# Block 0 of a two-part transformer kernel: input products from part products, paired attention scores and values, probabilities turned by a diagonal

## The chip, the core and the metric

The program runs on one core of one Trainium2 chip. The metric is the device time of one execution in microseconds, the median of several; lower is better. The engines are TensorE (PE in the profile, its weight loads PEld), VectorE (DVE), ScalarE (ACT), GpSimd (POOL) and SyncE (SP), which issues most DMAs. Each works through its own queue in order and waits on semaphores.

## The reference

256 tokens of width 1024 go through two blocks with a mixture of experts each, and then through a second model part (gated linear and forgetting attention, cross attention, MLP). All is float32. The change lies in block 0, before its experts:

```python
m   = ada_mod(c, ada_w[0], ada_b[0])                     # six vectors of 1024: silu(c) @ w + b
hn  = modulate(rms_norm(h, norm1_g[0]), m0, m1)          # latent rows, 256 x 1024
hcn = modulate(rms_norm(ctx, norm1_g[0]), mc0, mc1)      # context rows
proj = hn @ w_in                                         # 512 q | 128 k | 128 v | 512 u | 512 gate
q, k = rms_norm per head (64), rope;   v                 # 8 query heads, 2 key-value heads
k, v = concat(context k, v from hcn @ w_in[:, 512:768], own k, v)      # 512 keys
p    = softmax(q k^T / 8);   attn = p v                  # in blocks of 128 queries
g    = silu(layer_norm(depthwise_conv31(u * sigmoid(gate)) + b))
h    = h + m2 * (concat(attn, g) @ w_out)
```

Then the router of block 0 picks 32 tokens for each of 16 experts and the experts' weights (96 chunks of 2 MB) are streamed.

## The kernel before

**The ring.** All large weights pass through one ring of nine slots of 2 MB in SBUF, filled by SyncE in the order of `STREAM`. `load(i, ...)` (line 470) waits until chunk i-9 is used up, then issues the DMA. TensorE counts `chunks_used`. The order at the start is ada0a (4 chunks), u, gate, q, kv, ada0b, ada0c, ada1a, ada1b, ada1c (4 each), ev_out (2), then the experts. `arrived` waits for a chunk's DMA.

**Orders are written by hand.** Each engine has a function with its instructions in program order; what runs between what is fixed there. The numbers `TAPS_Q, TAPS_KV, TAPS_LOOP` and `LN_AT` say how many of the 124 convolution taps (31 taps on 4 channel groups) VectorE does in each place, and at which head the layer norm steps stand.

**Input products.** `transposes("x")` and `transposed` give the modulated input as columns xT. TensorE then multiplies in plain float32: u and gate to columns (`to_columns`, lines 1915 to 1922), q to rows (`to_rows`, 1907), the context is transposed, own and context k/v to rows (`kv_rows`, 2004). VectorE does gating, taps, context columns, then the norms of heads and rope (1305 to 1347). `ada(g, c, bank)` (1860 to 1873) multiplies one chunk of modulation weights, four narrow products side by side; group 1 stands before the attention, groups 2 to 5 inside its loop.

**Attention.** For each of 16 (block, head) pairs: `ev_scores` (2051), two ahead; VectorE takes the negated maximum; ScalarE the exponential with its sum; `ev_transposed` (2059) turns four 128x128 pieces by transposes; VectorE (even heads) or ScalarE (odd) copies them to SBUF as pT; `ev_values` (2066) multiplies pT, as the stationary operand, by 64 columns of values. `attn_rows` (1353) divides a block by its sums, and eight transposes (2112) turn the result to columns. `cv_sums` (2075), `ln_center`, `ln_inverse` and `ln_scale` are the layer norm of the convolution.

**Part products.** From ev_out on the kernel multiplies by parts: ScalarE rounds an operand to float32r (hi), VectorE or GpSimd subtracts (lo = x - hi), and `split_product` (1924) adds three products:

```python
for n, (x, y) in enumerate(((0, 1), (1, 0), (0, 0))):
    last = mm(out, lhs[x], rhs[y], start=start and n == 0, stop=stop and n == 2)
```

`ev_high` and `ev_low` make the halves of the ev_out chunks, through two buffers `evw_hi`. `low` (line 460) does it later in the kernel on either engine. `add_gated` adds the product to h, and `route` begins.

Of the kernel before, what the change touches and what calls it, by code (L numbers as in the profile page):

```python
# [5 lines left out]
F32 = mybir.dt.float32  # L6
# [6 lines left out]
P = 128  # L13
D = 1024
# [59 lines left out]
STREAM = [("ada0a", 4), ("ev_u", 1), ("ev_gate", 1), ("ev_q", 1), ("ev_kv", 1), ("ada0b", 4),  # L74
# [46 lines left out]
def build(nc, a):  # L121
    ctx = ExitStack()
    with ctx:
# [50 lines left out]
        def at(off, **dims):  # L174
# [5 lines left out]
            if len(dims) == 1:  # L180
# [9 lines left out]
        vall = at(7168, t=4, e=128)  # L190
# [4 lines left out]
        cwrow = at(8824, d=512)  # L195
# [4 lines left out]
        sq = rows_t[:, 0:1280].rearrange("p (t h e) -> p t h e", t=NT, h=10)  # L200
        sq_ctx = rows_t[:, 1280:1536].rearrange("p (t h e) -> p t h e", t=NT, h=2)
        ra, rb, rc, rd = (rows_t[:, 320 * j:320 * (j + 1)].rearrange("p (h e) -> p h e", h=10) for j in range(4))
# [4 lines left out]
        attn = xT_t[:, 0:1024].rearrange("p (t e) -> p t e", t=NT)  # L207
# [72 lines left out]

        evw_hi = [rows_hi.rearrange("p k n -> p (k n)"), parts_of("scratch", SLOT // 2, 5632)]
        ev_x = [[parts_of("scratch", 4 * N, first).rearrange("p (k n) -> p k n", k=4) for first in pair]
                for pair in ((1536, 7680), (2560, 3584))]
# [89 lines left out]
        SPLIT_INPUTS = ["ev_out", "mix1", "y", "mix2", "w_out", "xattn", "wo", "mlp"]  # L373
        NORM_BANKS = {n: (4, 5, 6, 7) for n in TRANSPOSED}
        NORM_BANKS["moe0"], NORM_BANKS["moe1"] = (4, 5, 2, 3), (0, 1, 2, 3)
# [24 lines left out]
        LN_AT = 10  # L400
        TAPS_Q, TAPS_KV, TAPS_LOOP = 35, 12, 8
# [33 lines left out]

        def ev_half(j, p):

            i, s = FIRST["ev_out"] + j, slice(SLOT // 2 * (1 - p), SLOT // 2 * (2 - p))
            return 2 * j + p, ring[:, slot_of(i), s], ring_r[slot_of(i)][:, s], evw_hi[p]
# [26 lines left out]
        def _(sp):  # L466
# [47 lines left out]
            sp.dma_start(ctx_rows, a["ctx"][0].rearrange("(t p) d -> p t d", p=P)).then_inc(sem("ctx_in"), 16)  # L514
            columns("ev_kv", evw, 1, width=256, col0=512)
            for g in range(1, len(ADA)):
                modulations(g)
# [40 lines left out]
        def _(act):  # L558
# [7 lines left out]
            act.wait_ge(sem("c_ps"), 1)  # L566
# [59 lines left out]

            act.wait_ge(sem("x_in"), 16)
# [8 lines left out]
            act.wait_ge(sem("ctx_in"), 16)  # L636
            squares("ctx", ctx_rows, by_token(flat(cT)))
# [4 lines left out]
            whole(act, "ev_gate")  # L642
            for j in range(2):
                nc.scalar.activation(flat(sg[:, 2 * j:2 * j + 2, :]), pb(6 + j), ACT.Sigmoid).then_inc(sem("cv_gate"), 1)

            whole(act, "ev_q")
# [5 lines left out]
            transposed("ctx", cT)  # L652
            for w, bank in ((0, 2), (1, 3)):
                if w:
                    whole(act, "ev_kv")
                else:
                    act.wait_ge(sem("own_kv"), 1)
# [6 lines left out]
                if not w:  # L664
                    act.wait_ge(sem("inverses"), 1)
# [10 lines left out]
            def ev_probs_T(m):  # L676
                act.wait_ge(sem("ev_pT_ps"), m + 1)
                if m >= 2:
                    act.wait_ge(sem("ev_pv"), m - 1)
                nc.scalar.activation(flat(pT[:, 1]), pb(5), ACT.Copy).then_inc(sem("ev_pT_act"), 1)  # L680

            for n in range(NT * NQ):
# [8 lines left out]
                if n == LN_AT:  # L691
                    act.wait_ge(sem("cv_centered"), 1)
                    nc.scalar.activation(flat(csq), flat(cacc), ACT.Square).then_inc(sem("cv_sq"), 1)
                if n == LN_AT + 1:
                    act.wait_ge(sem("inverses"), 3)
                    nc.scalar.activation(lnrow[:, :], lnrow[:, :], ACT.Sqrt).then_inc(sem("roots"), 1)
            ev_probs_T(NT * NQ - 1)
            def ev_high(j, p):

                n, w, lo, hi = ev_half(j, p)  # L700
# [1962 lines left out]
```

## Time and profile before

| | us |
|---|---|
| median of 3 runs (lowest, highest) | 1674.82 (1673.35, 1675.28) |
| the profiled execution, its own time | 1671.44 |
| its span (first to last instruction) | 1669.6 |
| PE busy | 1471.2 (88%) |
| DVE busy | 481.2 (29%) |
| ACT busy | 339.5 (20%) |
| POOL busy | 110.6 (7%) |

The granted TensorE clock is 0.966 of full speed over the span. HBM delivers 337 GB/s in the mean over the span, and 410 to 430 GB/s where the DMA engines are busy all the time. The rows below come from views of the profile: tables of stretches with the busy time of each engine, timelines (merged runs of equal instructions in order of time), groups of equal instructions, and lists of the durations of one line. Durations of TensorE instructions overlap, so the distance from one start to the next is the price of one, and the last one adds its tail.

### The profile page before, as it was taken

How to read it: one execution, taken by the hardware profiler on the slowest of the kernel's cores; microseconds unless marked ns; L12 is line 12 of the kernel's file. 1: busy time of each engine (PE TensorE's matmuls, PEld its weight loads, DVE VectorE, ACT ScalarE, POOL GpSimd, SP SyncE). 2: the span in 40 equal slices, each digit the busy share in tenths (PEclk: the TensorE clock that was granted, in tenths of full speed). 3: DMA queues.
4: the chain of work that ended last, by engine and by line, in shares of the span. 5: the costliest groups of instructions: out<-in, count | busy, mean ns of one | idle time of the engine just before them, and what ended most of it. 6: DMA issues, size and time to landing. Idle time of an engine off the chain costs nothing. (4 is left out here: it accounts for less than half of the span.)

```text
span 1669.6 us, 17591 instructions
## 1 busy us (share of the span) xinstructions
PE 1471.2 (88%) x7708; PEld 824.5 (49%) x7708; DVE 481.2 (29%) x732; ACT 339.5 (20%) x515; POOL 110.6 (7%) x109
## 2 busy tenths in 40 slices
PE   4999979889888899789798878978888999999999
PEld 2755642232232343289532323323324767788897
DVE  1496540100100000156500001001004754345443
ACT  1122410000000000143200000000003645544442
POOL 0000000000000000010000000000003044330000
PEclk9999989999989999999799999999999999999999
DMA  9989959999999999996399999999999844244510
GB/s 374 410 359 413 410 216 429 414 429 427 416 428 427 412 428 429 407 398 234 126 418 422 427 430 419 429 427 423 428 424 355 291 175 149 104 148 168 189 51 26
DMA packets 93298, 563.06 MB, mean 337 GB/s; under 512 B 8048, under 2 KB 9448, under 8 KB 53670
## 3 DMA queue, kind: packets, MB, share of 16 engines
q1 hardware_dynamic: 89504, 551.77, 81.2%
q0 software_dynamic: 2384, 9.42, 1.6%
q8 instruction: 61, 1.00, 0.2%
q10 hardware_dynamic: 1334, 0.75, 0.2%
q14 instruction: 15, 0.12, 0.0%
HBM read 558.74 MB, written 3.17 MB: 337 GB/s over the span
## 5 line engine op out<-in xcount | busy, mean ns | idle before, releaser
L2207 PE MATMUL ps<-ring,scratch 128*32 128x512 f32 x2048 | 434.6, 610 | 54.4 <-DMA ring<-in_moe_w_up 26.1
L2207 PEld LDWEIGHTS ps<-ring,scratch 128*32 128x32 f32 x2048 | 129.2, 112 | 346.7 <-issue 339.5
L2186 PE MATMUL ps<-ring,scratch 128*32 128x512 f32 x1024 | 205.8, 603 | 29.7 <-DMA ring<-in_moe_w_down 29.7
L1927 PE MATMUL ps<-ring_parts,scratch_parts 128*128 128x512 f32 x656 | 186.6, 402 | 5.0 <-DVE xT_parts L1189 1.4
L1927 PE MATMUL ps<-scratch_parts,ring_parts 128*128 128x256 f32 x704 | 146.0, 282 | 0.0
L1927 PEld LDWEIGHTS ps<-ring_parts,scratch_parts 128*128 128x128 f32 x656 | 122.4, 189 | 33.1 <-DVE xT_parts L1189 1.6
L2186 PEld LDWEIGHTS ps<-ring,scratch 128*32 128x32 f32 x1024 | 50.3, 111 | 160.8 <-issue 107.8
L607 ACT ACTIVATE ring_parts<-ring 128x2048 fp32r<-128x2048 f32 x56 | 106.4, 1919 | 93.1 <-PE ps L1927 86.6
L460 DVE TENSOR_TENSOR ring_parts<-ring,ring_parts 128x2048 fp32r<-128x2048 f32 x46 | 105.6, 2296 | 54.9 <-ACT ring_parts L607 53.8
L1927 PEld LDWEIGHTS ps<-scratch_parts,ring_parts 128*128 128x128 f32 x704 | 114.7, 189 | 0.3
L1519 DVE TENSOR_TENSOR scratch<-ps,gate_bc 128x512 f32<-128x512 f32 x16 | 11.1, 692 | 250.9 <-PE ps L2186 250.9
L1927 PE MATMUL ps<-xT_parts,ring_parts 128*128 128x256 f32 x288 | 80.5, 280 | 1.3 <-DVE xT_parts L1180 1.3
L2215 PE MATMUL ps<-scratch,rows 128*128 128x128 f32 x256 | 66.5, 421 | 13.1 <-DVE scratch L1548 5.6
L2215 PEld LDWEIGHTS ps<-scratch,rows 128*128 128x128 f32 x256 | 61.6, 327 | 31.2 <-issue 15.4
L1508 DVE TENSOR_TENSOR scratch<-scratch,ps 128x1024 f32<-128x1024 f32 x8 | 9.8, 1222 | 231.4 <-PE ps L2207 231.4
L1912 PE MATMUL ps<-ring,xT 128*128 128x512 f32 x160 | 72.9, 617 | 2.2 <-DVE xT L1168 2.2
L742 ACT ACTIVATE scratch<-ps,mod_cols,scale_cols 128x128 f32<-128x128 f32 x32 | 12.9, 453 | 277.8 <-PE ps L2215 277.8
L1927 PE MATMUL ps<-ring_parts,xT_parts 128*128 128x512 f32 x160 | 62.6, 391 | 0.0
L1504 DVE SCALAR_TENSOR_TENSOR scratch<-ps,cst,scratch 128x256 f32<-128x256 f32 x8 | 3.9, 484 | 188.2 <-ACT scratch L746 188.2
L1872 PE MATMUL ps<-ring,silu_c 128*32 128x512 f32 x384 | 49.3, 648 | 7.7 <-issue 6.8
L1927 PEld LDWEIGHTS ps<-xT_parts,ring_parts 128*128 128x128 f32 x288 | 54.6, 190 | 1.8 <-issue 1.5
L754 ACT ACTIVATE scratch<-ps 128x512 f32<-128x512 f32 x8 | 4.8, 597 | 245.7 <-PE ps L2241 245.7
(393 smaller groups left out, 1552.1 us busy)
## 6 DMA issues: line engine op xcount, KB each, us to landing
ring<-in_moe_w_gate SPq DMA_DIRECT2D x64, 2048.0 KB, 30.0
ring<-in_moe_w_up SPq DMA_DIRECT2D x64, 2048.0 KB, 17.9
ring<-in_moe_w_down SPq DMA_DIRECT2D x64, 2048.0 KB, 30.1
ring<-in_ada_w SPq DMA_DIRECT2D x24, 2048.0 KB, 15.3
ring<-in_mlp_w SPq DMA_DIRECT2D x16, 2048.0 KB, 8.7
ring<-in_sc_w_in SPq DMA_DIRECT2D x6, 2048.0 KB, 21.5
ring<-in_w_in SPq DMA_DIRECT2D x6, 2048.0 KB, 20.7
ring<-in_xattn_wkv SPq DMA_DIRECT2D x4, 2048.0 KB, 35.5
```

What stands on the lines that cost most here:

```text
L460: ops.tensor_tensor(lo, w, hi.bitcast(F32), ALU.subtract).then_inc(sem("w_split"), 1)
L607: nc.scalar.activation(hi, w, ACT.Copy).then_inc(sem("w_high"), 1)
L742: last = nc.scalar.activation(xsT[:, k, :], ps[:, GATHER[b], P * (k % 2):P * (k % 2 + 1)], ACT.Identity, scale=scale[:, k:k + 1], bias=shi ...
L754: nc.scalar.activation(flat(hT[:, 4:8, :]), pb(7), ACT.Copy).then_inc(sem("mo_hT_act"), 1)
L1508: nc.vector.tensor_tensor(hid, hid, ps[:, 2:4, :].rearrange("p b f -> p (b f)"), ALU.mult)\
L1519: nc.vector.tensor_tensor(ym[:, 512 * j:512 * j + 512], pb(4 + j), gate_bc[:, 512 * j:512 * j + 512], ALU.mult).then_inc(sem("mo_ym"), 1)
L1872: last = mm(ps[32 * j:32 * j + 32, bank, :], lhs, rhs, start=(c == k == 0), stop=(c == 3 and k == 1))
L1912: last = mm(ps[:, banks[t], col:col + width], lhs[:, k, P * t:P * (t + 1)], slot8(i)[:, k, 0:width], start=(k == 0), stop=(k == KD - 1))
L1927: last = mm(out, lhs[x], rhs[y], start=start and n == 0, stop=stop and n == 2)
L2186: last = mm(ps[32 * j:32 * j + 32, banks[half], :], src[:, k, CAP * j:CAP * (j + 1)], w[:, e, col:col + 512], start=(k == 0), stop=(k == K ...
L2207: last = mm(ps[32 * j:32 * j + 32, banks[half], :], src[:, k, CAP * j:CAP * (j + 1)], w[e][:, 0, col:col + 512], start=(k == 0), stop=(k = ...
L2215: last = mm(ps[:, GATHER[b], P * (k % 2):P * (k % 2 + 1)], run_slice(rows[:, t, :], k), onehot[:, t, P * g:P * (g + 1)], start=(t == 0), s ...
```

## The change

It works on block 0 before the experts alone. In words:

- u, gate, q and kv are multiplied by parts, in seven halves (`IN_HALVES`), each rounded by ScalarE (`in_high`) and subtracted by GpSimd (halves 0, 3, 4, 5, 6) or VectorE (1, 2). x and the context columns are split too, the context by GpSimd. u and gate go alternately by halves, so the first two channel groups of the convolution start after two halves; the taps are done by pairs of groups.
- kv comes after ada0b in the stream. ada group 2 is multiplied before the attention.
- Scores of two heads stand next to each other, on different row halves of the array. Probabilities are multiplied by a diagonal of the inverse sums instead of transposed, which turns and divides in one. Values are the stationary operand (64 columns) and pT the moving one; two heads go to different column halves, and the result is already in columns. `attn_rows` and the eight transposes go.
- The layer norm steps and the ev_out halves get new places; the half that multiplies the attention comes first.

```diff
-STREAM = [("ada0a", 4), ("ev_u", 1), ("ev_gate", 1), ("ev_q", 1), ("ev_kv", 1), ("ada0b", 4),
+STREAM = [("ada0a", 4), ("ev_u", 1), ("ev_gate", 1), ("ev_q", 1), ("ada0b", 4), ("ev_kv", 1),
...
-        LN_AT = 10
-        TAPS_Q, TAPS_KV, TAPS_LOOP = 35, 12, 8
+        TAPS_FIRST, TAPS_Q, TAPS_KV, TAPS_LOOP = 40, 26, 12, 7
+        MEAN_AT, CENTER_AT, SQUARE_AT, VAR_AT, ROOT_AT, SCALE_AT = 7, 8, 9, 12, 13, 14
+        ATTN_HIGH_AT, ATTN_LOW_AT, EV_HIGH_AT = 10, 11, 14
+        EV_HALVES = [(0, 1), (1, 1), (0, 0), (1, 0)]
+        IN_HALVES = [("ev_u", 0), ("ev_gate", 0), ("ev_u", 1), ("ev_gate", 1), ("ev_q", 0), ("ev_q", 1), ("ev_kv", 0)]
...
+        def in_low(eng, ops, n):
+            w, lo, hi = in_half(n)
+            eng.wait_ge(sem("in_high"), n + 1)
+            if n:
+                eng.wait_ge(sem("in_low"), n)
+            ops.tensor_tensor(lo, w, hi.bitcast(F32), ALU.subtract).then_inc(sem("in_low"), 1)
...  ScalarE
             squares("x", h, xT_rows)
+            in_high(0)
             transposed("x", xT)
+            pairs_high("x", xT, in_hi)
+            in_high(1)
...
+            in_high(2)
...
+            gates(0)
+            in_high(3)
+            in_high(4)
+            gates(1)
+            in_high(5)
+            in_high(6)
...  GpSimd
             rms("x")
+            in_low(pool, nc.gpsimd, 0)
             rms("ctx")
+            for n in range(3, len(IN_HALVES)):
+                in_low(pool, nc.gpsimd, n)
+            for b in range(4):
+                c = slice(2 * b, 2 * b + 2)
+                pool.wait_ge(sem("x_high"), 4 * SPLIT_INPUTS.index("ctx") + b + 1)
+                nc.gpsimd.tensor_tensor(in_hi[:, c, :], cT[:, c, :], xT_r[:, c, :].bitcast(F32), ALU.subtract)\
+                    .then_inc(sem("x_split"), 1)
...  VectorE, before the head norms
+            gated(0)
...
+            taps(TAPS_FIRST)
+            gated(1)
+            normed("ctx", ctx_rows, ctx_rows)
             dve.wait_ge(sem("gpad"), 2)
             taps(TAPS_Q)
+            in_done(dve, 6)
             transposed("ctx", cT)
-            taps(TAPS_KV)
...  VectorE, in the loop over heads
+            def weighted(n):
+                dve.wait_ge(sem("ev_p"), n + 1)
+                if n >= 2:
+                    dve.wait_ge(sem("ev_pT_ps"), n - 1)
+                link(nc.vector.reciprocal(sm[:, 112 + n:113 + n], sm[:, 96 + n:97 + n]))
+                nc.vector.tensor_scalar(diag[:, n % 2, :], ident, sm[:, 112 + n:113 + n], None, ALU.mult)\
+                    .then_inc(sem("ev_diag"), 1)
...
-                taps(TAPS_LOOP)
+                taps(3)
+                weighted(n)
+                taps(TAPS_LOOP - 3)
...  TensorE
+            half_used(in_columns(0, 4))
+            half_used(in_columns(1, 6))
...
+            used(in_columns(2, 5))
+            used(in_columns(3, 7))
+            pe.wait_ge(sem("norm_ss"), 4)
+            half_used(in_rows(4))
+            used(in_rows(5))
             pe.wait_ge(sem("gpad"), 2)
             pe.wait_ge(sem("cv_gate"), 2)
             transposes("ctx", ctx_rows)
...
+            half_used(kv_rows(2, (in_hi, xT_r)))
             for c in range(4):
                 ada(1, c, 3)
+            pe.wait_ge(sem("ev_rows"), 2)
+            input_split("ctx")
+            used(kv_rows(0, (xT_r, in_hi)))
+            for c in range(4):
+                ada(2, c, 7)
...
                 for s in range(4):
-                    last = nc.tensor.transpose(ps[:, 4 + n % 2, P * s:P * (s + 1)], pexp[:, n % 2, P * s:P * (s + 1)], ident)
+                    last = mm(ps[:, 4 + n % 2, P * s:P * (s + 1)], pexp[:, n % 2, P * s:P * (s + 1)], diag[:, n % 2, :],
+                              start=True, stop=True)
...
                 for s in range(4):
-                    last = mm(ps[:, 6 + t, 64 * (n % 8):64 * (n % 8) + 64], pT[:, w, s, :], vall[:, s, 64 * w:64 * w + 64],
-                              start=(s == 0), stop=(s == 3))
+                    for m in (n, n + 1):
+                        t, i, w = ev_head(m)
+                        o, k = 64 * (i % 2), 2 * w + i // 2
+                        last = mm(ps[o:o + 64, 6 + t, P * k:P * (k + 1)], vall[:, s, 64 * w:64 * w + 64], pT[:, w, s, :],
+                                  start=(s == 0), stop=(s == 3))
...
             for n in range(NT * NQ):
                 ev_transposed(n)
+                if n % 2 == 0:
+                    if n + 2 < NT * NQ:
+                        ev_scores(n + 2)
+                        ev_scores(n + 3)
+                    if n:
+                        ev_values(n - 2)
...
+                if n == MEAN_AT:
+                    cv_sums(0)
+                if n == VAR_AT:
+                    cv_sums(1)
```

## Rows read from the trace of the kernel before

**Rows 1.** Table of stretches: length, busy us (instructions) per engine, PE clock, DMA share, GB/s
```profile
240.00:260.00 20.00, 19.06 (x104) 7.49 (x105) 0.73 (x2) 0.81 (x2) 0.00 (x0) 1.00 1.00 425
220.00:240.00 20.00, 11.43 (x59) 7.01 (x59) 10.79 (x30) 1.50 (x6) 0.00 (x0) 0.74 0.40 120
191.00:213.50 22.50, 22.50 (x100) 18.16 (x99) 12.37 (x14) 5.47 (x5) 0.00 (x0) 1.00 0.79 319
```

**Rows 2.** Timeline of TensorE: start us, length us, what; one product is two instructions
```profile
36.76 14.05 PE L1920 MATMUL ps<-xT,ring 128*128 128x256 f32 x64 [2.65 <-ACT xT L592]
...
95.36 3.64 PE L1872 MATMUL ps<-ring,silu_c 128*32 128x512 f32 x32 [0.88 <-ACT scratch L663]
```

**Rows 3.** Timeline of TensorE in the attention
```profile
105.62 1.95 PE L2056 MATMUL ps<-scratch 64*128 64x512 f32 x6 [0.40 <-DVE scratch L1351]
...
136.62 0.66 PE L2064 MATMUL ps<-cst,scratch 128*128 128x128 f32 x4
137.11 1.00 PE L2071 MATMUL ps<-scratch 128*128 128x64 f32 x8
...
140.76 1.12 PE L2056 MATMUL ps<-scratch 64*128 64x512 f32 x2
...
163.43 1.95 PE L2084 MATMUL ps<-scratch,ones 128*128 128x256 f32 x8
...
170.22 0.66 PE L2064 MATMUL ps<-cst,scratch 128*128 128x128 f32 x4 [0.22 <-ACT scratch L686]
...
187.91 1.09 PE L2112 MATMUL ps<-cst,xT 128*128 128x128 f32 x8 [1.08 <-DVE xT L1359]
```

**Rows 4.** Timeline of TensorE, part products of 256 columns late in the kernel
```profile
1285.35 0.28 PE L1927 MATMUL ps<-xT_parts,ring_parts 128*128 128x256 f32 x1
...
1285.70 0.28 PE L1927 MATMUL ps<-xT_parts,ring_parts 128*128 128x256 f32 x1
```

**Rows 5.** Line 470, issue of the u chunk: ns min/median/max, start; landing after it
```profile
L470 SPq DMA_DIRECT2D ring<-in_ev_w_in x1: 3916/3916/3916, 7.1 to 7.1; - x1
...
DMA to landing us min/median/max: 27.0/27.0/27.0
```

**Rows 6.** Timeline of ScalarE, a rounding
```profile
181.91 1.90 ACT L706 ACTIVATE rows_parts<-ring 128x2048 fp32r<-128x2048 f32 x1
```

**Rows 7.** Subtractions by line: ns min/median/max, first and last start us
```profile
L460 DVE TENSOR_TENSOR ring_parts<-ring,ring_parts x46: 2229/2292/2595, 1277.4 to 1650.7; 128x2048 fp32r<-128x2048 f32 x46
L460 POOL TENSOR_TENSOR ring_parts<-ring,ring_parts x10: 4558/4578/4623, 1385.9 to 1477.8; 128x2048 fp32r<-128x2048 f32 x10
...
L1607 DVE TENSOR_TENSOR xT_parts<-xT,scratch_parts x4: 678/680/1780, 712.7 to 715.6; 128x512 fp32r<-128x512 f32 x4
```

**Rows 8.** Timeline of VectorE: taps, squares of the head norms, squares for the context
```profile
68.65 12.35 DVE L1294 SCALAR_TENSOR_TENSOR scratch<-scratch 128x256 f32<-128x256 f32 x31
...
88.43 1.49 DVE L1313 TENSOR_TENSOR rows<-scratch 128x1280 f32<-128x1280 f32 x1 [0.87 <-ACT scratch L663]
...
100.71 0.42 DVE L1313 TENSOR_TENSOR rows<-scratch 128x256 f32<-128x256 f32 x1
```

**Rows 9.** Timeline of GpSimd around two meetings with VectorE
```profile
709.36 4.52 POOL L1071 TENSOR_TENSOR ring_parts<-ring,scratch_parts 128x2048 fp32r<-128x2048 f32 x1 [0.93 <-DVE rows L1155]
...
1284.53 1.44 POOL L1030 TENSOR_TENSOR rstd<-ms,mhalf 128x1 f32<-128x1 f32 x1
```

**Rows 10.** Timeline of VectorE at the same two places
```profile
712.65 1.78 DVE L1607 TENSOR_TENSOR xT_parts<-xT,scratch_parts 128x512 fp32r<-128x512 f32 x1 [0.93 <-ACT scratch_parts L823]
...
1284.28 1.28 DVE L1650 SCALAR_TENSOR_TENSOR h<-h,rstd,scratch 128x1024 f32<-128x1024 f32 x1 [1.45 <-POOL rstd L1030]
```

**Rows 11.** Groups by form: busy us, mean ns of one, idle before
```profile
L2375 PE MATMUL ps<-scratch 64*128 64x128 f32 x16 | 1.2, 285 | 0.0
...
L2354 PE MATMUL ps<-cst,ms 128*128 128x128 f32 x4 | 0.6, 273 | 0.0
```

**Rows 12.** Table of stretches, one us in the attention's start
```profile
114.00:115.00 1.00, 1.00 (x8) 0.20 (x4) 1.00 (x4) 0.00 (x0) 0.00 (x0) 0.50 0.95 397
```

More of the change, by code:

```diff
@@ L194, in build @@
         cw = at(9848, c=CT, j=34)
-        cwrow = at(8824, d=512)
+        cwrow = at(9336, d=512)
         grow = at(9336, i=P)
@@ L1276, in _, with gated @@
             link(nc.vector.memset(gpad[:, :, edge + N:PADW], 0.0))
-            whole(dve, "ev_u")
-            for j in range(2):
+            def gated(j):
+                in_done(dve, (0, 2)[j])
                 dve.wait_ge(sem("cv_gate"), j + 1)
@@ L1419, in _ @@
-            ev_low(0, 1)
-            mod_cols(5, 3)
-            nc.vector.tensor_copy(router_bias, ps[:, 2, 0:E])
+            ev_low(0, 1)
+            attn_low(1)
+            ev_low(1, 1)
+            dve.wait_ge(sem("mo_shift"), 1)
+            nc.vector.tensor_copy(router_bias, ps[:, 2, 0:E])
+            ev_low(0, 0)
+            for b in range(2):
+                hi, lo = (flat(v[:, 2 * b:2 * b + 2, :]) for v in ev_x[0])
+                dve.wait_ge(sem("x_high"), 4 * SPLIT_INPUTS.index("ev_out") + 2 + b + 1)
+                nc.vector.tensor_tensor(lo, flat(cacc[:, 2 * b:2 * b + 2, :]), hi.bitcast(F32), ALU.subtract)\
+                    .then_inc(sem("x_split"), 1)
@@ L1914, in to_rows @@
                 return last
-            def to_columns(i, rhs, banks):
-                for c in range(4):
-                    for k in range(KD):
-                        last = mm(ps[:, banks[c // 2], N * (c % 2):N * (c % 2 + 1)], slot8(i)[:, k, P * c:P * (c + 1)],
-                                  rhs[:, k, :], start=(k == 0), stop=(k == KD - 1))
-                return last
             def split_product(out, lhs, rhs, start, stop):
@@ new lines, in in_rows @@
+            def in_rows(n):
+                w, lo, hi = in_half(n)
+                pe.wait_ge(sem("in_low"), n + 1)
+                half = IN_HALVES[n][1]
+                for t in range(NT):
+                    s = slice(P * t, P * (t + 1))
+                    for kk in range(4):
+                        k, c = 4 * half + kk, slice(512 * kk, 512 * kk + 512)
+                        last = split_product(pb(t), (in_hi[:, k, s], xT_r[:, k, s]), (hi[:, c], lo[:, c]), k == 0, k == KD - 1)
+                return last
@@ new lines, in _, with ev_product @@
+            ev_values(NT * NQ - 2)
+            def ev_product(j, p, t):
+                n, w, lo, hi = ev_half(j, p)
+                pe.wait_ge(sem("w_split"), n + 1)
+                s = slice(P * t, P * (t + 1))
+                for k in range(4):
+                    c = slice(512 * k, 512 * k + 512)
+                    if p or k % 2 == 0:
+                        input_split("ev_out", t if p else 2 + k // 2)
+                    last = split_product(pb(((0, 1), (4, 5))[j][t]), (ev_x[p][0][:, k, s], ev_x[p][1][:, k, s]),
+                                         (hi[:, c], lo[:, c]), p == 1 and k == 0, p == 0 and k == 3)
+                return last
```

326 lines of the change are left out of this document (170 added, 156 removed).

## Prediction

> **What bounds the kernel now.** I read the table of stretches first, then the timelines of TensorE, VectorE, ScalarE and GpSimd in block 0, then single groups for the prices. Weights stream through a ring of nine slots. From 240 us on the DMA engines are busy all the time and move 425 GB/s, but from 220 to 240 only 0.40 of it [rows 1]: the ring is full and TensorE has not yet reached the first experts. So the end of block 0 sets when the stream goes on, and each microsecond that TensorE reaches the experts later or earlier goes unshortened to the end. Until then TensorE is nearly always busy: input products from 36.8 us, the next ada group at 95.4, attention until 186.8, the ev_out product from 191.0 to 213.5 [rows 1 to 3]. The forecast is the shift of that last number. It is made on the profiled execution (span 1669.6, own time 1671.4 us) and put on the median of 1674.82, 3.4 us above it.
>
> **Input products.** Now a product of 256 columns costs 14.05/32 = 0.439 us (each is two passes) [rows 2], one of 512 twice that. Three part products of 256 columns repeat every 0.35 to 0.36 us (1285.35, 1285.70) [rows 4]; the 96 part products of 512 columns of ev_out took 22.5 us [rows 1], 0.70 for three. So u and gate take 11.5 us each (14.05), q 11.2 (14.0), k and v of both inputs 11.5 (14.05). Sum 45.7 instead of 56.2: TensorE is owed 10.5 us.
>
> What must come first is new. The u chunk lands at 7.1 + 27.0 = 34.1 us [rows 5]. Then ScalarE rounds a half, 1.9 us like L706 [rows 6], and GpSimd subtracts it: 4.58 us per 128x2048 half, where VectorE takes 2.29 [rows 7]. First half: 34.1, 36.0, 40.6. The parts of x are ready beside it, their subtractions on VectorE after 40.6 (below). TensorE starts at 41.3 instead of 36.8. From there each half (5.76 us) follows the one before by: product done, sigmoid, rounding 1.9, GpSimd 4.6. That fits with stalls of 1 and 2 us before halves 3 and 5, and they end at about 80.5.
>
> **The term that decides: VectorE beside GpSimd.** The subtractions of halves 3 to 6 run on GpSimd between about 57 and 80 us, exactly where VectorE has its convolution taps, each with two inputs in SBUF, 12.35/31 = 0.40 us apart [rows 8]. In the trace these don't run side by side. GpSimd's subtraction of 709.36 ends at 713.88; VectorE's 128x512 subtraction of 712.65 takes 1.78 us, the other three of its line 0.68 [rows 7, 9, 10]: it ended 0.55 after GpSimd let go. The other way round, a scalar_tensor_tensor of VectorE at 1284.28 (1.28 us, the same operation as a tap) ended at 1285.56, and a GpSimd power of 128x1 that began inside it, at 1284.53, took 1.44 and ended 0.41 after it [rows 9, 10]. So one waits for the whole of the other. No row shows a tap waiting for GpSimd, so the bounds are 0 and more than full exclusion; I take exclusion with turns, since two of the three ingredients are measured. The Trainium skill ("SBUF — State Buffer", section "Who interferes with whom") is wider than the rows: any VectorE instruction with two SBUF inputs contends with a GpSimd instruction that reads SBUF, and the one that comes first keeps the port for its whole length. By it the taps wait; without it the sum would be the first rival's.
>
> Four times 4.58 = 18.3 us are so added to VectorE. Its work from 55.9: 40 taps 16.1 us with 18.3 of waits end at 90; second gating product and the two normed context rows 2.0 (an estimate from 128x512 at 0.68 [rows 7]), at 92. TensorE's context transposes wait for both (gpad 2, norm_rows), and with them its whole queue: idle from 80.5 to 91.5. Then transposes 1.9, own k/v 5.8 and about 1.7 for a clock that has fallen, at 100.9; ada group 1 8.2, at 109. VectorE does 26 taps to 102.6, then the context columns to 104.5; ScalarE rounds them and GpSimd subtracts four 128x512 pieces (4.58/4 each) against the squares of the head norms, ready 110.6; context k/v at 116.4, ada group 2 at 124.6. VectorE's head norms and rope, 12.3 us now (88.4 to 100.7) [rows 8], run 104.5 to 118 with these waits, then 12 taps 4.8 and the context norms 2.5: 125.3. Some 5 us on, as now between the end of the norms and the first turned head (103.2 and 108.3), that head is turned: 130.6 instead of 108.3. **Term: 22.3 late.** At nothing: kv moved four chunks later in SP's queue and the early ada group 2, since DMA has a store of chunks by then; the hole that it had near 90 us only moves.
>
> **Attention.** Per head: turning now takes four transposes, 0.49 us to the next instruction (136.62 to 137.11) [rows 3]. A product by the diagonal is eight passes of 128 columns; four such passes took 0.6 us with a last one of 0.27, so 0.11 apart, 0.88 per head [rows 11]: +0.39 x 16 = +6.2. Scores: two alone 2 x 1.05 (1.12 with its tail), as a pair in two row halves about 0.95 (pair and single took 1.95 [rows 3]); seven pairs save 7 x 1.1 = 7.7, less one already paired, 6.7. Values: 0.94 per head now (1.00 with its tail) [rows 3]; the pair has 16 passes in two column halves, two row halves of the same size took 1.2 for 16 [rows 11], so 1.0 per pair: 8 x 0.88 = 7.0 saved. Were column halves not concurrent it would be 1.7 to 1.9 per pair and nothing saved; four column groups did overlap (32 ada passes of 512 columns in 3.64 us [rows 2], 0.114 each, where one alone needs 0.43), and I take concurrent. The Trainium skill ("TensorE: Matmul & The Clock Gate", Part 3, "The mechanism") says that weight loads overlap only where the row group differs, which would cost those 7 us here; the ada row contradicts it. One ada group is gone from the loop, 8.5, the fourth turn of its columns is +0.6. Reciprocal and diagonal put 0.45 us per head on VectorE, and seven taps fewer wait: 4.3 us per head against TensorE's 4.1, a loss of 1.
>
> New wait at the end: the sums of the squares stand at head 12, with no ada work behind them. Their end (now 165.38) frees row statistics, a root, the load of the exponential's table and the next exponential before a head can be turned (now 170.22): 4.84 us, of which TensorE waits 0.22, since ada and values lie beside it [rows 3]. After the change it is 5.4 with inverse and diagonal, and TensorE has 0.9 of work in it. Then the rounding of the first ev_out half (1.9) stands before exponential 15. TensorE waits 7.0 in all, and the clock, which is 0.5 at 114 to 115 after the idle time of 110 to 112 [rows 12], costs 1.5. Sum of the loop: 78.5 now; +6.2 -6.7 -7.0 -8.5 +0.6 +1 +7.0 +1.5 = 72.6, rounded 72. **Term: -6.4.**
>
> **After attention.** The final 8 transposes and their wait, 186.8 to 188.8 [rows 3], go; the router's shift stays. The ev_out product, 22.5 us, begins with the half that needs no convolution; rounding (1.9) and subtraction (2.3) of each later half fit within the 5.6 us of a half. 24.4 instead of 26.7: **-2.3**.
>
> **Sum:** 22.3 - 6.4 - 2.3 = +13.6. Block 0 ends at 227 instead of 213.5; route and experts are the same and the ring is full either way, so the end moves by 13.6: 1688.4 us.
>
> **Rivals.** (1) GpSimd does not hold the taps up. Then VectorE finishes its 66 taps at 84.3, TensorE starts the first head at 115, the first term is +6.7 and the sum -2.0 to -3.5 (with the fall of the clock or without): 1672. For it: no tap has stood beside GpSimd so far, and 40 and 26 taps fit this case, with VectorE idle for 2.7 us; against it: the rows above. It ends faster or the same by whether more than 3.35 us is gained, which pairing by columns and the clock decide; if the start is also 2 us shorter it is 1669. (2) The port doesn't take turns: back-to-back taps keep GpSimd out until VectorE stops. Then the subtractions of halves 3 and 5 start only after 40 and 26 taps, and TensorE waits for them: 12 to 13 us more, 1701. For it: the order of arrival decides in the rows and taps leave no gap; against it: VectorE's subtraction waiting at 712.65 came at once. (3) Exclusion, and paired values don't overlap: 7 us on top, 1695.
>
> **Chances.** Exclusion with turns 0.58, with (3) 0.08 on top of it; starved GpSimd 0.12; no exclusion 0.22, of which 0.14 faster. A measurement of this kernel can tell 0.2%, 3.35 us, from no change. Faster 0.14, same 0.08, slower 0.78. Terms of the likeliest are good for 5 us either way: 1683 to 1694. For eight in ten the range reaches from half of the first rival to the second: 1671 to 1700.
>
> **What would show it.** Taps of 4 us and more among those of 0.48 on VectorE between 55 and 85 us, their number equal to the GpSimd subtractions; TensorE idle for 8 to 12 us before the context transposes; first turned head near 130. If GpSimd's subtractions keep 4.6 us beside taps of 0.48, the exclusion is wrong, and the kernel is near 1672. A turned head of 0.9 us, pairs of scores and values near 1.0, 5 us of idle time before head 14, and the expert stream shifted by the same amount as the end show the rest; a DMA stall after 250 us that wasn't there, or a shift at the end other than that of the ev_out product, would refute the rigid shift.

## The result

| | us |
|---|---|
| before, median of 4 runs beside it (lowest, highest) | 1674.09 (1672.29, 1675.28) |
| after, median of 4 runs (lowest, highest) | 1706.66 (1702.79, 1708.16) |
| ratio, 95% interval | 1.0191 [1.0179, 1.0203] |
| span of the profiled execution, before and after | 1669.6 and 1706.3 |
| granted TensorE clock over the span, before and after | 0.966 and 0.951 |

The change makes the kernel slower by 32.6 us, where 13.6 were forecast. The direction was right, and so was the forecast that VectorE and GpSimd exclude each other. Who waits for whom was right for half of the subtractions only, the late landing of the parameters was missing, and the attention was sized too cheap: the time lies above the range.

### The profile page after: what moved, and what is told of

It is laid out like the page before. It is cut to its first block and busy times, and to the rows that moved or that the text cites. A ratio compares the mean times of both kernels' runs of the same rounds, so it can differ in the third digit from the quotient of the medians.

```text
span 1706.3 us, 18024 instructions
## 1 busy us (share of the span) xinstructions
PE 1474.4 (86%) x7876; PEld 837.7 (49%) x7876; DVE 508.2 (30%) x764; ACT 357.6 (21%) x530; POOL 150.3 (9%) x118
## 5 line engine op out<-in xcount | busy, mean ns | idle before, releaser
L2019 PE MATMUL ps<-ring_parts,scratch_parts 128*128 128x512 f32 (+1 forms) x672 | 193.0, 402 | 15.3 <-POOL ring_parts L475 10.3
L2019 PE MATMUL ps<-scratch_parts,ring_parts 128*128 128x256 f32 x768 | 166.3, 285 | 0.0
L2019 PEld LDWEIGHTS ps<-ring_parts,scratch_parts 128*128 128x128 f32 x672 | 126.7, 191 | 44.1 <-issue 8.7
L2019 PEld LDWEIGHTS ps<-scratch_parts,ring_parts 128*128 128x128 f32 x768 | 129.2, 192 | 0.3
L1619 DVE TENSOR_TENSOR scratch<-ps,gate_bc 128x512 f32<-128x512 f32 x16 | 11.1, 692 | 251.2 <-PE ps L2311 251.2
L2019 PE MATMUL ps<-ring_parts,xT_parts 128*128 128x512 f32 (+1 forms) x192 | 74.3, 387 | 1.9 <-POOL scratch_parts L1117 1.9
L2012 PE MATMUL ps<-ring,xT 128*128 128x512 f32 x128 | 55.6, 594 | 2.2 <-DVE xT L1253 2.2
```

The costliest lines, as they stand in the source:

```text
L1619: nc.vector.tensor_tensor(ym[:, 512 * j:512 * j + 512], pb(4 + j), gate_bc[:, 512 * j:512 * j + 512], ALU.mult).then_inc(sem("mo_ym"), 1)
L2012: last = mm(ps[:, banks[t], col:col + width], lhs[:, k, P * t:P * (t + 1)], slot8(i)[:, k, 0:width], start=(k == 0), stop=(k == KD - 1))
```

## The profile after

First the stretches, whose columns are those of [rows 1].

```profile
225.80:248.30 22.50, 22.50 (x106) 18.59 (x106) 11.90 (x12) 8.92 (x11) 0.00 (x0) 1.00 0.19 68
220.00:240.00 20.00, 19.22 (x94) 15.83 (x94) 7.56 (x8) 11.23 (x12) 0.00 (x0) 0.86 0.03 11
260.00:280.00 20.00, 15.07 (x78) 8.44 (x82) 8.94 (x23) 0.81 (x2) 0.00 (x0) 0.75 0.38 140
```

The ev_out product ends at 248.3 instead of 213.5 [rows 1]: 34.8 us late, against 36.7 in the span. As before, the ring is full and the DMA engines rest while TensorE comes to the experts. They rest longer, at 0.03 from 220 to 240. In the profiles of the kernels before and after and of the variants below, what follows the transposes of h behind ev_out (215.2 before, 250.0 after) takes 1452 to 1457 us. So the shift is rigid within 5 us, which is little beside 35 us, and much beside the small differences between the later variants.

Next, who TensorE waited for between 36 and 250 us: in all, times, longest.

```profile
PE ps L2185 <- DVE gate_bc L1458: 12.5, 6, 4.5
PE ps L2019 <- POOL ring_parts L475: 10.3, 2, 7.1
PE ps L2132 <- DMA cst<-in_cst: 9.4, 1, 9.4
PE ps L2019 <- DVE xT_parts L1354: 5.7, 1, 5.7
PE ps L2019 <- POOL scratch_parts L1117: 1.9, 1, 1.9
```

The timeline of TensorE has the places of the second and third row, and the first turned head:

```profile
62.92 0.63 PE L2132 MATMUL ps<-cst,scratch 34*128 34x34 f32 x4 [9.36 <-DMA cst<-in_cst]
...
64.08 0.41 PE L2019 MATMUL ps<-scratch_parts,rows_parts 128*128 128x256 f32 x1
...
69.01 0.28 PE L2019 MATMUL ps<-scratch_parts,rows_parts 128*128 128x256 f32 x1
...
84.50 0.76 PE L2019 MATMUL ps<-ring_parts,scratch_parts 128*128 128x512 f32 x1 [7.07 <-POOL ring_parts L475]
103.00 0.58 PE L2019 MATMUL ps<-ring_parts,scratch_parts 128*128 128x256 f32 x1 [3.24 <-POOL ring_parts L475]
...
139.76 1.47 PE L2185 MATMUL ps<-gate_bc,scratch 128*128 128x128 f32 x8 [2.33 <-DVE gate_bc L1458]
145.99 1.16 PE L2185 MATMUL ps<-gate_bc,scratch 128*128 128x128 f32 x8 [1.84 <-DVE gate_bc L1458]
...
212.88 2.07 PE L2185 MATMUL ps<-gate_bc,scratch 128*128 128x128 f32 x8 [4.47 <-DVE gate_bc L1458]
214.88 1.98 PE L2199 MATMUL ps<-scratch 128*64 128x128 f32 x16
218.11 2.07 PE L2185 MATMUL ps<-gate_bc,scratch 128*128 128x128 f32 x8 [1.25 <-DVE gate_bc L1458]
220.96 1.98 PE L2199 MATMUL ps<-scratch 128*64 128x128 f32 x16 [0.78 <-ACT scratch L753]
```

The first head is turned at 139.76 instead of 108.31: 31.4 late, forecast 22.3. The loop, from there to 222.9, takes 83.2 us instead of 78.5, forecast 72. What follows to 248.3 takes 25.4, forecast 24.4. The granted clock is 0.81 from 54 to 100: behind the wait that ends at 62.9, the part products start 0.21 us apart until 68.8 and 0.12 us apart from there.

Now GpSimd and VectorE in the same time, where the forecast put its first term. GpSimd:

```profile
56.07 4.50 POOL L475 TENSOR_TENSOR ring_parts<-ring,scratch_parts 128x2048 fp32r<-128x2048 f32 x1 [2.25 <-ACT scratch_parts L677]
73.88 10.48 POOL L475 TENSOR_TENSOR ring_parts<-ring,rows_parts 128x2048 fp32r<-128x2048 f32 x1 [13.31 <-ACT rows_parts L677]
84.50 4.82 POOL L475 TENSOR_TENSOR ring_parts<-ring,scratch_parts 128x2048 fp32r<-128x2048 f32 x1
94.55 8.40 POOL L475 TENSOR_TENSOR ring_parts<-ring,rows_parts 128x2048 fp32r<-128x2048 f32 x1 [5.23 <-ACT rows_parts L677]
```

VectorE:

```profile
64.85 15.15 DVE L1383 SCALAR_TENSOR_TENSOR scratch<-scratch 128x256 f32<-128x256 f32 x38
79.89 0.70 DVE L1370 TENSOR_TENSOR scratch<-ps,scratch 128x512 f32<-128x512 f32 x1
80.50 9.37 DVE L1240 TENSOR_SCALAR scratch<-scratch,rstd 128x1024 f32<-128x1024 f32 x2
89.79 8.79 DVE L1383 SCALAR_TENSOR_TENSOR scratch<-scratch 128x256 f32<-128x256 f32 x22
98.50 4.92 DVE L1386 TENSOR_SCALAR scratch<-scratch 128x256 f32<-128x256 f32 x2
```

The subtraction of 56.07 has VectorE idle beside it and takes 4.50. The one of 73.88 falls into a run of taps that keep their 0.40 us, and it ends at 84.36, 4.5 us after the last of them: it did nothing for 6 us. The one of 94.55 ends 4.5 us after the taps' end at 98.5. In return two rows of VectorE that take 0.75 us each alone stretch to 9.37, and two small ones to 4.92, each over one or two subtractions. So the two engines exclude each other as forecast, but these runs of taps do not give turns. This is the second rival's mechanism, for two of the four subtractions of halves 3 to 6.

## Experiments

Each median is one of 4 to 10 runs, beside the kernel before, whose medians were 1673.56 to 1673.87. "First head" is the start of the first turned head in the profile; it is also 119.6 in e6 and 117.5 in e4, which have the same instructions up to there, so 2 us of it mean nothing.

| | first head | median (lowest, highest) | ratio, interval |
|---|---|---|---|
| after | 139.8 | 1706.66 (1702.79, 1708.16) | 1.0191 [1.0179, 1.0203] |
| e1 parameters early | 133.9 | 1702.49 (1696.35, 1704.54) | 1.0166 [1.0146, 1.0187] |
| e2 subtractions on VectorE | 130.2 | 1698.55 (1697.95, 1700.34) | 1.0151 [1.0135, 1.0166] |
| e3 both | 126.0 | 1691.41 (1690.27, 1692.44) | 1.0104 [1.0087, 1.0121] |
| e10 e3, fewer taps first | 118.2 | 1681.08 (1677.06, 1684.43) | 1.0045 [1.0025, 1.0065] |
| e4 attention alone | 117.5 | 1683.30 (1682.09, 1685.18) | 1.0059 [1.0044, 1.0074] |
| e5 e4, columns late | 119.1 | 1680.33 (1679.79, 1681.39) | 1.0043 [1.0028, 1.0058] |
| e6 e4, transposes | 119.6 | 1675.09 (1673.69, 1677.06) | 1.0010 [1.0001, 1.0020] |
| e7 e4, ada group in the loop | 118.5 | 1684.92 (1683.16, 1686.61) | 1.0069 [1.0052, 1.0086] |
| e8 e7 and e5 | 116.4 | 1686.29 (1684.14, 1687.05) | 1.0076 [1.0061, 1.0091] |
| e9 e8, taps placed | 110.8 | 1676.92 (1676.37, 1680.89) | 1.0026 [1.0014, 1.0039] |
| e12 e9, diagonal first | 111.0 | 1678.33 (1673.75, 1680.30) | 1.0032 [1.0020, 1.0043] |

### Where the start goes: e1, e2, e3

e1 moves the seven parameter transfers:

```diff
             squares("x", h, xT_rows)
+            act.wait_ge(sem("params_ps"), 2)
+            act.dma_start(cwrow[0:CONVK, :], a["ev_conv_w"][0])...     # and the six others
             in_high(0)
...
             in_high(1)
-            act.dma_start(cwrow[0:CONVK, :], a["ev_conv_w"][0])...     # and the six others
```

> The changed kernel with ScalarE issuing the seven parameter transfers (convolution weights and rows, head gains, rotation table) ahead of its first rounding, at about 26 us instead of 38.7 to 41.2 us, so ahead of the four 2 MB modulation chunks. Theory late landing: TensorE's wait of 9.4 us at 53.5 goes and everything behind is 9 us earlier: block 0 ends at 239, about 1697.5 us. Theory port (VectorE's taps, read from and written to SBUF one behind another, keep GpSimd off): the taps now begin at 55 and GpSimd's subtraction of half 3 waits for the end of the 40 taps at 70, so that product of half 3 is later than in the changed kernel (about 75 instead of 70.4), the own keys' product still starts at 103 to 105, and the time is 1706 to 1709 us.

TensorE's wait of 9.4 us is gone and the first head is 5.9 us earlier. The time gains 4.2 us, between the two theories and matching neither. The port theory's picture was wrong in a way that tells more. The taps from 58.76, by line of VectorE (ns min, median, max), and GpSimd's subtractions:

```profile
L1384 DVE SCALAR_TENSOR_TENSOR scratch<-scratch x38: 472/476/4828, 58.8 to 90.8; 128x256 f32<-128x256 f32 x38
```
```profile
58.92 4.76 POOL L475 TENSOR_TENSOR ring_parts<-ring,scratch_parts 128x2048 fp32r<-128x2048 f32 x1 [2.26 <-ACT scratch_parts L677]
64.74 4.87 POOL L475 TENSOR_TENSOR ring_parts<-ring,rows_parts 128x2048 fp32r<-128x2048 f32 x1 [1.06 <-ACT rows_parts L677]
72.19 4.92 POOL L475 TENSOR_TENSOR ring_parts<-ring,scratch_parts 128x2048 fp32r<-128x2048 f32 x1 [2.57 <-ACT scratch_parts L677]
```

Here GpSimd came in at once all four times (the fourth, at 77.61, took 4.64), and the 38 taps took 32.5 us instead of 15.15: four waits, together 17 us, with single taps of up to 4.83. That is the picture that the forecast drew. TensorE then waits 9.7 us before the context transposes for the context's rows, which stand behind the taps. Either way VectorE and GpSimd exclude each other; only the loser differs. The rest of the edit's worth went there and to the start: ScalarE's first rounding begins 2.7 us later (35.16 instead of 32.43), behind a u chunk that lands later.

e2 takes GpSimd out:

```diff
-            for n in range(3, len(IN_HALVES)):            # GpSimd
-                in_low(pool, nc.gpsimd, n)
...
-            taps(TAPS_FIRST); gated(1); normed("ctx", ...)    # VectorE
-            taps(TAPS_Q)
+            in_low(dve, nc.vector, 3); taps(22); in_low(dve, nc.vector, 4); taps(9)
+            in_low(dve, nc.vector, 5); gated(1); normed("ctx", ...); taps(4)
+            in_low(dve, nc.vector, 6); taps(31)
```

> The changed kernel with the subtractions of halves 3 to 6 on VectorE (about 2.3 us each), put between its taps, instead of on GpSimd; all else is the same. Theory port: the waits of TensorE for the lower parts (7.1, 2 and 3.2 us) go, the own keys' product starts at about 93 instead of 103, block 0 ends near 238 and the time is 1696 to 1698 us. Theory late landing alone: the products of halves 4 to 6 had no need of the port; less than 3 us gained, 1704 us or more, since VectorE has 9 us of work more.

8.1 us come back, though VectorE has 9.2 us of work more. The subtractions take 2.29 and the taps 0.40 each; TensorE's waits for lower parts fall from 10.3 us to 0.8. The context transposes start at 87.2 instead of 97.9, 1.6 us of it because the parameters happened to be there at 61.3 instead of 62.9. Some of that is lost again: the context's columns wait for the last 31 taps, and TensorE waits 6.1 us for the context's lower parts (1.9 before).

e3 has both edits, with the same 66 taps cut up in another way around the subtractions (3, 12, 12, 5 and 34 instead of 22, 9, 4 and 31).

> Both edits: parameter transfers early and the subtractions of halves 3 to 6 on VectorE. If the late landing and the port are separate causes that hide one another: the own keys' product starts at about 84, block 0 ends near 229, time about 1687 us, far more than the two edits gain apart from each other. If they are not, no more than the better of the two alone (1696 us). The forecast of 1688.4 had neither the late landing nor this much starving, so it would be met here.

15.3 us, somewhat more than the 12.3 of the two alone, not the 20 expected. Each edit gives something that the other does not, and a third cause stands behind them:

```profile
54.00:100.00 46.00, 41.32 (x305) 32.64 (x303) 44.05 (x86) 17.95 (x24) 5.08 (x6) 0.99 0.99 394
```

From 54 to 100 VectorE is busy 44.05 of 46 us; in the kernel before it was 33.31. TensorE's longest wait after 54 us is now 7.57 us, for the context's lower parts, whose columns stand behind 34 taps. (At the start it waits 8.8 us for the first lower parts of x, 5.7 in the changed kernel: that is the price of the early parameters.) e10 tests this:

```diff
-            in_low(dve, nc.vector, 6); taps(34)
+            in_low(dve, nc.vector, 6); taps(20)
-        TAPS_LOOP = 7;  MEAN_AT, CENTER_AT, SQUARE_AT = 7, 8, 9
+        TAPS_LOOP = 8;  MEAN_AT, CENTER_AT, SQUARE_AT = 8, 9, 10      # and the edit of e5
```

> The kernel of e3 with fourteen of its 78 taps ahead of the attention moved into the loop (8 a head instead of 7, the convolution's sums one head later) and the modulation columns behind the diagonal as in e5. Theory VectorE full: in e3 VectorE is busy 44 of the 46 us from 54 to 100, and its taps hold up the context's columns; now they are ready at 90, the first turned head comes at 121 instead of 126, and with 3 us from e5's edit the time is about 1683 us. Rival, loads: DMA is at 0.99 of its time in that stretch of e3 and the modulation weights set it; only e5's 3 us show, 1688 us.

The first head comes at 118.2 and the time falls by 10.3 us, more than expected; e5's edit, part of it, was worth 3.0. The DMA share is 1.00 from 54 to 100 here too, so the loads did not hold the 7 us that came. This is the whole change with its parameter transfers, subtractions and taps in new places, 25.6 us faster than as it stood, and its first head is as early as with plain products (e4). It is also no faster than plain products with the same attention and e5's edit (1680.33): the 10.5 us that part products were to save TensorE are not seen, and 9.2 us of wait for x's first lower parts stand at its start.

> The changed kernel once more, unchanged. In its first profile GpSimd waited for VectorE's taps at halves 4 and 6 (10.5 and 8.4 us for a subtraction of 4.5), while in e1 VectorE waited for GpSimd each time. If the outcome is fixed by the program, both long subtractions are seen again; if it is drawn anew in each execution, one or both are 4.5 to 5 us and the taps show the stall.

One execution, 1706.24 us, and the same picture, the two long subtractions within 0.2 us:

```profile
74.27 10.63 POOL L475 TENSOR_TENSOR ring_parts<-ring,rows_parts 128x2048 fp32r<-128x2048 f32 x1 [13.59 <-ACT rows_parts L677]
85.05 4.84 POOL L475 TENSOR_TENSOR ring_parts<-ring,scratch_parts 128x2048 fp32r<-128x2048 f32 x1
94.93 8.58 POOL L475 TENSOR_TENSOR ring_parts<-ring,rows_parts 128x2048 fp32r<-128x2048 f32 x1 [5.04 <-ACT rows_parts L677]
```

So within this program the loser repeats. Across programs it doesn't: e1 turned it round by moving some DMAs. What decides who waits stays open. Whether it changes between runs of e1, which spread over 8.2 us, was not seen, since only one was profiled; a wide spread alone says little, for e10, where GpSimd does none of these halves, has 7.4.

### What the attention costs: e4 to e9, e12

e4 has plain float32 input products in the changed order of work:

```diff
-            last = split_product(..., (hi[:, k, s], lo[:, k, s]), (in_hi[:, k, :], xT_r[:, k, :]), ...)
+            last = mm(..., w[:, k, s], xT[:, k, :], ...)      # no in_high, in_low, pairs_high
```

> The changed kernel with block 0's input products in plain float32 again (no rounding, no subtractions), but its attention, its order of loads and its tail as changed. Theory loop dearer than forecast: first turned head near 108 to 112, loop of 83 us, then 25.4 us: block 0 ends at 217 to 221, so 1677 to 1681 us, slower than before. By the forecast's loop of 72 us it would end at 205 and the time would be 1665 us.

9.7 us slower than before, 2 us above the range of the first theory (the profiled span, 1680.7, is 11.1 above that of before). So the new attention is itself a loss, and the part products add the other 23.4. The first head is 9.2 late, and the second ada group now stands ahead of it (103.8 to 111.7). The loop then takes 81.6 us instead of 78.5, though it has that group no more. Its waits for the diagonal are those of the whole change, 12.5 us in six. The end of its loop:

```profile
183.58 1.05 PE L2159 MATMUL ps<-gate_bc,scratch 128*128 128x128 f32 x8
189.10 2.08 PE L2159 MATMUL ps<-gate_bc,scratch 128*128 128x128 f32 x8 [4.47 <-DVE gate_bc L1434]
191.11 1.98 PE L2173 MATMUL ps<-scratch 128*64 128x128 f32 x16
194.35 2.08 PE L2159 MATMUL ps<-gate_bc,scratch 128*128 128x128 f32 x8 [1.26 <-DVE gate_bc L1434]
197.20 1.98 PE L2173 MATMUL ps<-scratch 128*64 128x128 f32 x16 [0.78 <-ACT scratch L744]
```

Three waits, and behind the first one every price is nearly doubled: the granted clock is 0.60 from 185 to 200, where full speed alternates with the lower level of 1.2 GHz.

This run also tells where the changed kernel's wait of 9.4 us for parameters comes from. The stream of chunks has the new order here too, but ScalarE has no rounding to do ahead of the seven parameter transfers. Their last issue, in the changed kernel and then in e4, and what VectorE waits for in e4:

```profile
40.80 0.45 ACTq L696 DMA_DIRECT2D cst<-in_cst  x1
```
```profile
36.47 0.45 ACTq L693 DMA_DIRECT2D cst<-in_cst  x1
48.27 0.20 DVE L1336 TENSOR_SCALAR gate_bc<-gate_bc 128x64 f32<-128x64 f32 x1 [12.04 <-DMA cst<-in_cst]
52.07 0.43 PE L2106 MATMUL ps<-cst,scratch 34*128 34x34 f32 x4
```

Issued 4.3 us earlier, they land 14.6 us earlier, at 48.3 instead of 62.9, and TensorE turns the convolution's weights at 52.1 without a wait (50.7 in the kernel before). So the new order of chunks alone does not make them late; the roundings that now stand ahead of their issue on ScalarE do.

```diff
-                if n % 4 == 1:
-                    mod_cols(2 + n // 4, 3)
                 taps(3)
                 weighted(n)
+                if n % 4 == 1:
+                    mod_cols(2 + n // 4, 3)
```

> The kernel of e4 (attention alone), with VectorE's modulation columns of steps 1, 5 and 9 behind the head's reciprocal and diagonal instead of ahead of them. Theory VectorE's order: TensorE's waits for the diagonal at heads 1, 5 and 9 (1.84, 2.00 and 0.65 us in e4) go: 1679 us against 1683.3. Rival: the wait only moves to the modulation product that follows, which needs these columns: 1683 us.

3.0 us come back, as the first theory said in size, but not by its mechanism: the waits at heads 1, 5 and 9 only fall to 1.46, 1.85 and 0.57 us, one of 0.82 is new at head 2, and the waits for the diagonal are 12.8 us in all, against 12.5 in e4. What differs in the profiles is the granted clock. First e4, then e5:

```profile
117.00:135.00 18.00, 15.64 (x112) 7.70 (x116) 15.61 (x43) 3.15 (x8) 1.54 (x3) 0.91 1.02 421
185.00:200.00 15.00, 8.86 (x50) 7.54 (x51) 7.13 (x11) 6.93 (x11) 0.00 (x0) 0.60 0.95 401
```
```profile
117.00:135.00 18.00, 13.61 (x108) 7.27 (x112) 16.63 (x44) 3.60 (x9) 1.54 (x3) 1.00 1.01 420
185.00:200.00 15.00, 8.57 (x54) 7.30 (x55) 7.95 (x11) 7.92 (x11) 0.00 (x0) 0.77 1.02 431
```

Over the whole span the clock is 0.957 to 0.961 in e4's four runs and 0.962 to 0.964 in three of e5's four (0.957 in the fourth). How moving the columns brings this about is not shown.

```diff
-                    last = mm(ps[...], pexp[:, n % 2, P * s:P * (s + 1)], diag[:, n % 2, :], start=True, stop=True)
+                    last = nc.tensor.transpose(ps[...], pexp[:, n % 2, P * s:P * (s + 1)], ident)
```

This kernel leaves out the division by the sums of the probabilities, so it prices the product with the diagonal and is not a version that could be used.

> The kernel of e4 with TensorE's four transposes by the identity in place of the four products with the diagonal; VectorE still makes the diagonal and TensorE still waits for it, so only the price of the pass changes (the division by the sums of the probabilities is left out of the computation). Theory dearer pass: 1.16 us a head turned becomes 0.65, as in the kernel before, 8 us over 16 heads, less what the tail's waits swallow: 1675 to 1678 us. Rival: VectorE's chain sets the pace in the loop, and the gain is under 2 us: 1681 us or more.

```profile
152.14 0.66 PE L2159 MATMUL ps<-cst,scratch 128*128 128x128 f32 x4
152.63 1.89 PE L2185 MATMUL ps<-scratch,ones 128*128 128x256 f32 x8
```

8.2 us. A turned head costs 0.49 to the next start here and 1.09 with the diagonal; 16 times 0.60 is 9.6, of which 8.2 reach the end. What a kernel with transposes would pay for dividing elsewhere was not run.

e7 takes the second ada group into the loop again (`ada(2, c, 7)` ahead of it goes, the loop runs `ada(2 + n // 4, c, 3)` up to head 15, the last columns follow the first ev_out product).

> The kernel of e4 with the second modulation group's products taken from ahead of the attention back into it, so that the last group lies beside heads 13 to 15 as in the kernel before. Theory empty tail: the first turned head comes 8 us earlier (109 instead of 117.5), the loop grows by less than that, since the waits and the half clock of 185 to 200 are filled: 1676 to 1678 us. Rival: VectorE's chain sets the tail, which then stays as it is, and the 8 us are only moved: 1683 us.

The tail filled as expected: one group more, and the loop takes 82 us as in e4. But the first head did not come 8 us earlier. It came at 118.5, behind this wait of TensorE:

```profile
112.06 1.11 PE L2137 MATMUL ps<-cst,scratch 128*128 128x128 f32 x4 [4.52 <-DVE scratch L1395]
```

It is for the context's head norms, which VectorE does behind twelve taps; the ada group had hidden them. The time is near the rival's 1683 and not the theory's 1676 to 1678, for a reason that neither named.

> The kernel of e4 with both edits of order (modulation columns behind the diagonal, second group back in the loop). If both causes are real and apart: 1672 to 1675 us, so no slower than the kernel before. If VectorE's chain is the bound: 1680 us or more.

No gain from the pair in the time: 1686.3. The first heads stand in half clock (2.08 us a turned head, twice), and the order ahead of the attention still binds. In the profiles block 0 does end earlier than in e7, its transposes of h at 226.8 instead of 230.2, but what follows takes 1457.3 us instead of 1453.3, so the time says nothing about the pair that is finer than 4 us.

```diff
-        TAPS_Q, TAPS_KV = 26, 12
+        TAPS_Q, TAPS_KV = 38, 0
```

> The kernel of e8 (attention alone, both edits of order) with the twelve taps that stand between the rotation and the context's head norms (4.8 us on VectorE, and TensorE waits 4.5 us behind them) put into VectorE's idle stretch at 83 to 90. Theory VectorE ahead of the attention: the first turned head comes at 112 instead of 116.4 and the time is 1680 us or less, against 1686.3. Rival: something else holds the first head (loads of the modulation weights, the context product), and the time stays above 1684 us.

```profile
105.77 0.66 PE L2137 MATMUL ps<-cst,scratch 128*128 128x128 f32 x4 [1.46 <-DVE scratch L1395]
...
110.76 1.16 PE L2158 MATMUL ps<-gate_bc,scratch 128*128 128x128 f32 x8 [2.33 <-DVE gate_bc L1433]
```

9.4 us for moving twelve taps into an idle stretch: 1676.9, or 3.4 us above the kernel before in the same set. That VectorE's order ahead of the attention held the first head is shown: it comes 5.6 us earlier. The whole 9.4 us are not its worth. In the profiles the transposes of h start 4.7 us earlier (222.1 instead of 226.8), and the other 4.9 us of the two spans lie behind block 0, where the kernels are the same: there TensorE waits 71 us for the experts' weights, and 83 in e8. Why is open.

```diff
-                taps(3)
+                taps(1 if n == 0 or n % 4 == 1 else 3)
                 weighted(n)
```

> The kernel of e9 with one tap instead of three ahead of the reciprocal and diagonal of heads 0, 1, 5, 9 and 13, and three taps fewer in head 0. In e9 TensorE waits 2.33, 2.14, 1.76, 0.67 and 2.62 us for these diagonals, 9.5 us in all. Theory VectorE's order: a tap takes 0.40 us, so heads 0, 1, 5 and 9 give back some 3 us: 1674 us, level with the kernel before. Rival: the diagonal waits for ScalarE's exponential and not for the taps, so nothing comes: 1677 us.

No gain: the intervals of e9 and e12 overlap. In the profile the wait at head 1 (2.14) is gone and that at head 0 is 2.08 instead of 2.33, where VectorE now waits 0.46 us for ScalarE's exponential; a new one of 1.61 stands at head 6, so 8.0 us are left of 9.5. The profiled span is 2.6 us shorter than e9's (1671.9), the median 1.4 longer: an effect of this size is lost in the spread of the seven runs, and the experiment does not settle it. No version tried beats the kernel before.

## Why the prediction was right and wrong

**Slower, by the port.** The term that decides was the right one to look at: VectorE and GpSimd exclude each other, TensorE stands idle for it, and e2 gives 8.1 us back. But the step "exclusion with turns" held for no subtraction of the changed kernel that met taps: at 73.88 and 94.55 GpSimd waited for the run of taps, and not the taps for GpSimd.

The Trainium skill ("SBUF — State Buffer", section "Who interferes with whom") was right where the rows of before were silent: the taps do contend, and one instruction waits for the whole of the other. It also says that the first to issue keeps the port. Taken plainly, the subtraction then comes in behind one tap of 0.40 us, as in all four cases of e1; at 73.88 it waited 6 us, some 15 taps. Why a whole run of taps kept the port in one program and yielded at every arrival in another is in no run here.

**First term, 22.3 forecast, 31.4 measured.** Two errors of unequal kind. The forecast had TensorE wait 11 us in one piece for VectorE. It waited in two, 7.07 and 3.24, for GpSimd: equal in size by luck. What failed outright is that every change to the loads was put "at nothing", for the reason that DMA has a store of chunks: the sum looked at the chunks, and had no term for the seven parameter transfers. ScalarE issues them between 38.7 and 41.2, behind its new roundings, instead of from 34.6 to 37.1. By then SyncE is issuing 8 MB of ada chunks, from 34.2 to 40.7, and the last small transfer lands at 62.9, 22 us after its issue. TensorE needs it, to turn the convolution's weights, at 53.5. These 9.4 us are about the difference between 22.3 and 31.4. e1 and e4 show that the time of issue decides, with the new order of chunks in both; whether they would be late with the old order and the late issue was not run. e1 also shows that the 9.4 us can be had back only in part, since VectorE's queue stands behind them.

**Loop, 72 forecast, 83.2 measured.** (The forecast's terms add up to 72.6; its -6.4 takes 72.1.) Mis-sized terms: the turn costs 1.09 and not 0.88, 16 x 0.21 = 3.4 us (e6 confirms the price); pairs of scores 1.06 and not 0.95, 0.8 us in seven; the waits at heads 1, 5 and 9 cost 4.5 us where 1 was put; half clock doubles two turns and two pairs of values in the tail, 3.6 us where 1.5 was put. These are 9.8 of the 11.2; the rest lies in half-clock pieces behind the waits of heads 1 and 5. The tail's waits are right: 4.47, 1.25 and 0.78 make 6.5, forecast 7.0.

**Right.** Pairs of values in column halves overlap: 16 passes in 1.03 to 1.09 us, forecast 1.0, so the third rival falls. The forecast had read 7 us more out of a sentence of the Trainium skill ("TensorE: Matmul & The Clock Gate", Part 3, "The mechanism"), that weight loads overlap with running products only where the row group differs; these pairs use all 128 rows, so the same row groups, and the trace shows no such price. After the loop 25.4, forecast 24.4. The shift is rigid within 5 us.

**The sum.** -0.5 was forecast for the attention (the ada group's 8.2 ahead of it, -6.4, -2.3) and e4 has 9.7; 14.1 was forecast for the part products and the order around them, and what e4 leaves is 23.4. At the end of block 0 the misses are 9.1 in the first term, 11.2 in the loop and 1.0 behind it, 21.3 us; the median shows 19.0 of them. The forecast's own value for TensorE's share, that part products save it 10.5 us, was not wrong at full clock, where three of 256 columns take 0.35 us in the trace too; but TensorE was not the end of the chain ahead of the attention, and the waits also cost it clock.

**The rivals' places.** The starved GpSimd had 0.12 and the price 1701. It came for half of the subtractions, and TensorE's waits for them, 10.3 us, stood in place of the 11 us of the likeliest case and not 12 to 13 us on top of it. The range stopped at this rival alone; no case held a late landing together with dearer heads.

## What to carry to other kernels

Before TensorE's saved passes get a value, add up the work that they put on the engine beside it in that stage: VectorE was at 33 of 46 us here, and much of what was added was paid. Ask of every instruction put ahead of a DMA's issue what else is being issued by then: here 4.3 us of rounding on ScalarE put seven small transfers behind bulk on SyncE's queue, and they landed 14.6 us later. Work that stands ahead of a chain may hide another engine's order; before it is moved, look at what is late next.

## What the hardware showed that was not expected

- Seven small transfers (none above 64 KB) whose last is issued at 40.80 on ScalarE's queue, while SyncE issues four chunks of 2 MB from 34.2 to 40.7, have landed at 62.9; in e4, with the last issued at 36.47 and SyncE's chunks from 34.9 to 41.8, they have landed at 48.3.
- A run of two-input instructions on VectorE can keep a GpSimd subtraction off for 6 us (10.48 instead of 4.50), and in another program the same pair goes the other way round four times of four (38 taps in 32.5 us instead of 15.15).
- In the run that keeps GpSimd off, it is let in at an instruction of VectorE with one input in PSUM (79.89); the next VectorE instruction, from SBUF to SBUF with one tensor input, then waits for the whole subtraction (9.37 us for two of 0.75).
- Eight passes of 128 columns against the diagonal cost 1.09 us, four transposes of the same pieces 0.49.
